# A decoder layer on one core: the sample rows' new SSM states by one product of 96 rounded rows instead of a full fp32 product of 64 rows

## The reference, cut to what matters

```python
xdt = (xs.astype(f32) * dt[..., None]).reshape(bsz, nc, chunk, g, r, p)
bc = bm.astype(f32).reshape(bsz, nc, chunk, g, n)
decay_states = jnp.exp(cs[..., -1:] - cs)
states = jnp.einsum('bcsgn,bgrcs,bcsgrp->bcgrpn', bc, decay_states, xdt)
...
new_states = jnp.einsum('bgrzc,bcgrpn->bzgrpn', decay_chunk, states)
final = new_states[:, -1].reshape(bsz, nh, p, n).astype(h0.dtype)
```

## Time and profile before

| | |
|---|---|
| median of 3 runs | 2976.16 us (2974.51 to 2977.68) |
| the profiled execution | 2979.95 us |
| its span | 2978.2 us |
| TensorE (PE) busy | 2927.1 us, 98% |
| VectorE (DVE) busy | 1876.1 us, 63% |
| ScalarE (ACT) busy | 881.1 us, 30% |
| GpSimd (POOL) busy | 1233.2 us, 41% |
| stage with the scan's steps | about 1770 to 2515 us of the span |

### The profile page before, as it was taken

One profiled execution on the slowest core, in us unless ns is written; L12 is line 12 of the kernel. 1 busy time (PEld: TensorE's weight loads), 2 busy tenths in 40 slices (PEclk: granted clock), 3 DMA queues, 4 the chain that ended last, 5 costly groups with the idle time before them and its releaser, 6 DMA issues.

```text
span 2978.2 us, 51636 instructions
## 1 busy us (share of the span) xinstructions
PE 2927.1 (98%) x22164; PEld 2787.5 (94%) x22164; DVE 1876.1 (63%) x2050; ACT 881.1 (30%) x1411; POOL 1233.2 (41%) x575
## 2 busy tenths in 40 slices
PE   6999999999999999999999999999999999999998
PEld 4898899999999999999999999999999989999886
DVE  3303788898885889979886756686667755111302
ACT  3121222333233333333322233233333343211322
POOL 1133344444433444444444554443444534444332
PEclk9999999999999999999999999999999999999999
DMA  8878886664356886656667666666657665866643
GB/s 330 343 271 336 317 295 240 226 208 152 126 175 209 293 297 228 212 223 255 233 235 272 234 221 215 214 218 242 214 193 242 224 212 194 310 249 236 254 176 141
DMA packets 221035, 704.82 MB, mean 237 GB/s; under 512 B 26932, under 2 KB 130604, under 8 KB 171372
## 3 DMA queue, kind: packets, MB, share of 16 engines
q1 hardware_dynamic: 158262, 471.33, 45.2%
q0 software_dynamic: 5248, 174.60, 14.5%
q10 hardware_dynamic: 57296, 55.59, 5.6%
HBM read 630.85 MB, written 245.17 MB: 294 GB/s over the span
## 4 chain that ended last, share of the span: by engine, by line
PE 92%; DMA 4%; DVE 2%; issue 1%; ACT 0%; SPq 0%; POOL 0%; DVEq 0%; ACTq 0%; POOLq 0%
PE acc L1432 25%; PE acc L1434 24%; PE acc L1433 24%; DMA w_raw<-in_w_in_t 1%; PE ps_s L1301 1%; PE ps_s L1595 1%; DMA w_raw<-in_w_ada_t 1%; PE ps_s L1561 1%; PE ps_t L1446 1%; PE ps_s L1680 1%; PE ps_s L1681 1%; PE ps_s L1682 1%; DMA side<-in_keys_t 1%; PE ps_s L1582 1%; PE acc L1680 0%
## 5 line engine op out<-in xcount | busy, mean ns | idle before, releaser
L921 POOL TENSOR_TENSOR w_lo<-w_raw,w_hi 128x1024 fp32r<-128x1024 f32 (+1 forms) x416 | 1094.5, 2650 | 1697.7 <-ACT w_hi L980 1697.7
L1432 PE MATMUL acc<-act,w_hi 128*128 128x288 f32 x5744 | 1717.8, 299 | 2.7 <-POOL w_lo L921 2.6
L1434 PE MATMUL acc<-act,w_lo 128*128 128x288 f32 x5744 | 1692.9, 295 | 0.0
L1433 PE MATMUL acc<-act,w_hi 128*128 128x288 f32 x5744 | 1692.6, 295 | 0.0
L1432 PEld LDWEIGHTS acc<-act,w_hi 128*128 128x128 f32 x5744 | 1078.9, 188 | 37.2 <-issue 26.8
L1433 PEld LDWEIGHTS acc<-act,w_hi 128*128 128x128 f32 x5744 | 1079.3, 188 | 1.1
L1434 PEld LDWEIGHTS acc<-act,w_lo 128*128 128x128 f32 x5744 | 1078.5, 188 | 0.0
L980 ACT ACTIVATE w_hi<-w_raw 128x1024 fp32r<-128x1024 f32 (+1 forms) x418 | 403.9, 1015 | 482.6 <-PE acc L1434 193.0
L1889 DVE TENSOR_TENSOR side<-side 128x2048 f32<-128x2048 f32 x96 | 274.5, 2859 | 81.9 <-DMA side<-in_vals_t 67.7
L1860 DVE TENSOR_TENSOR side<-side 128x2048 f32<-128x2048 f32 x96 | 269.9, 2811 | 81.2 <-DMA side<-in_keys_t 77.5
L1055 ACT ACTIVATE ev<-acc 128x576 f32<-128x576 f32 x112 | 72.9, 651 | 617.7 <-PE acc L1434 617.5
(11 more groups left out here) (355 smaller groups left out, 2757.8 us busy)
## 6 DMA issues: line engine op xcount, KB each, us to landing
w_raw<-in_w_in_t SPq DMA_DIRECT2D x160, 1024.0 KB, 7.8
out_s_kv<-in_cache_a_w POOLq DMA_DIRECT2D x80, 1632.0 KB, 9.2
side<-in_keys_t SPq DMA_DIRECT2D x52, 1024.0 KB, 7.9
side<-in_vals_t SPq DMA_DIRECT2D x52, 1024.0 KB, 7.9
out_s_kv<-in_cache_a_w POOLq DMA_DIRECT2D x24, 1344.0 KB, 8.1
w_raw<-in_w_ada_t SPq DMA_DIRECT2D x24, 1024.0 KB, 7.4
w_raw<-in_w_gate_t SPq DMA_DIRECT2D x16, 1024.0 KB, 10.2
w_raw<-in_w_o_b_t SPq DMA_DIRECT2D x16, 1024.0 KB, 7.7
```

What stands on the lines that cost most here:

```text
L921: nc.gpsimd.tensor_tensor(dst, raw[:, SLOT[s], ks, 0:cols], wh[:, u % 2, ks, 0:cols].bitcast(F32), ALU.subtract).then_inc(lo, 1)
L1432: nc.tensor.matmul(out, wh[:, c, k, 0:cols], high, start=(k == 0), stop=False)
L1433: nc.tensor.matmul(out, wh[:, c, k, 0:cols], low, start=False, stop=False)
L1434: mm = nc.tensor.matmul(out, wl[:, c, k, 0:cols], high, start=False, stop=(k == kt - 1))
```

## The change

It replaces the fp32 product of 64 rows by one fp32r product of 96 rows for 4 sequences (32 sample rows) at a time. The stationary side `xst` holds three blocks of 32 rows: rounded xds, its rest, rounded xds. The moving side `Bm` (now in `stacked`) holds rounded B, rounded B, rest of B. So one product sums high*high, low*high and high*low.

- ScalarE, step 2: one more copy of the samples' B, rounded, into `B_high`; step 6: a rounded copy of `xds` (32x512) and two 32x256 copies into `xst`, behind a wait on `xe`; step 11: two more 32x256 copies, behind a wait on `sn_t`.
- GpSimd, step 4: two 32x512 operations instead of one 64x1024.
- VectorE, step 5 (nothing stood there): `rows_of_B` (a 64x128 difference and four 32x512 products with the mask) and `sample_inputs` (two 32x256, in place of the 64x256 of step 6); steps 7 and 11: `low_rows`, a 32x256 difference, behind a wait on ScalarE's copies.
- TensorE: the same 32 products in the same places, now with waits on `xst_l` (VectorE's `low_rows`), `bm` and `bd`. `states_new` is called ahead of the other branches of its step, which no other branch shares; its place in the row stays.

```diff
-        Bm = side[0:SAMP, 1920:2944].rearrange("p (b n) -> p b n", b=NB)
+        Bm = stacked[0:96, :].rearrange("p (a b n) -> p a b n", a=2, n=P)
+        xds = side[96:P, 1920:2432].rearrange("p (a h q) -> p a h q", a=2, h=4)
+        xds_high = stacked[96:P, 512:1024].rearrange("p (a h q) -> p a h q", a=2, h=4)
...
+        xst = pairs[0:96, :].rearrange("p (a h q) -> p a h q", a=2, h=2)
+        B_high, B_low = lse[0:SAMP, :].bitcast(F32R), Bt[0:SAMP, 0, :].bitcast(F32R)
...
-                    nc.gpsimd.tensor_tensor(Bm, Bt[0:SAMP, 0, :].unsqueeze(1).broadcast_to((SAMP, NB, P)),
-                                            owner.unsqueeze(2).broadcast_to((SAMP, NB, P)), ALU.mult).then_inc(bm, 1)
-                    pool.wait_ge(bm, g + 1)
+                    for a in range(2):
+                        nc.gpsimd.tensor_tensor(Bm[32 * a:32 * a + 32, a], own_rows(B_high, a).bitcast(F32), own_mask(a), ALU.mult).then_inc(bm, 1)
+                    pool.wait_ge(bm, 2 * g + 2)
...
-                    after(act_e, bm, g)
+                    if i == 0:
+                        after(act_e, bm, 2 * g)
+                        after(act_e, bd, 5 * g)
+                        nc.scalar.activation(B_high, X[0][0:SAMP, 2 * P:3 * P], ACT.Copy)
...
+                if o in (6, 11):
+                    j = o // 11
+                    if j == 0:
+                        act_e.wait_ge(xe, 5 * g + 1)
+                        nc.scalar.activation(xds_high, xds, ACT.Copy)
+                    else:
+                        act_e.wait_ge(sn_t, 4 * g + 2)
+                    for rows in (slice(0, 32), slice(64, 96)):
+                        mm = nc.scalar.activation(xst[rows], xds[:, :, 2 * j:2 * j + 2, :], ACT.Copy)
+                    mm.then_inc(xst_h, 1)
...
-                pe.wait_ge(xe, 5 * g + 1)
-                pe.wait_ge(bm, g + 1)
+                j, half = k // 2, k % 2
+                pe.wait_ge(xst_l, 2 * g + j + 1)
+                pe.wait_ge(bm, 2 * g + 2)
+                pe.wait_ge(bd, 5 * g + 5)
...
-                nc.tensor.matmul(Z, xds[:, 2 * j:2 * j + 2, :].rearrange("p h q -> p (h q)"),
-                                 Bm[:, 4 * half:4 * half + 4, :].rearrange("p b n -> p (b n)"), start=True, stop=True).then_inc(sn_t, 1)
+                nc.tensor.matmul(Z, xst[:, half].rearrange("p h q -> p (h q)"),
+                                 Bm[:, half].rearrange("p b n -> p (b n)"), start=True, stop=True).then_inc(sn_t, 1)
...
+            def sample_inputs(g):
...
+                dve.wait_ge(e4, 5 * g + 1)
+                after(dve, sn_t, 4 * g)
+                for a in range(2):
+                    rows = slice(32 * a, 32 * a + 32)
+                    mm = TT(xds[:, a], xdt[rows, 0], de4[rows, :].unsqueeze(2).broadcast_to((32, 4, 64)), ALU.mult)
+                mm.then_inc(xe, 1)
+
+            def rows_of_B(g):
+
+                dve.wait_ge(bt, 5 * g + 1)
+                TT(B_low, Bt[0:SAMP, 0, :], B_high.bitcast(F32), ALU.subtract).then_inc(bd, 1)
+                after(dve, sn_t, 4 * g)
+                for a in range(2):
+                    TT(Bm[32 * (1 - a):32 * (1 - a) + 32, a], own_rows(B_high, a).bitcast(F32), own_mask(a), ALU.mult).then_inc(bd, 1)
+                dve.wait_ge(bd, 5 * g + 1)
+                for a in range(2):
+                    TT(Bm[64:96, a], own_rows(B_low, a).bitcast(F32), own_mask(a), ALU.mult).then_inc(bd, 1)
+
+            def low_rows(g, j):
+
+                dve.wait_ge(xst_h, 2 * g + j + 1)
+                TT(xst[32:64], xds[:, :, 2 * j:2 * j + 2, :], xds_high[:, :, 2 * j:2 * j + 2, :].bitcast(F32), ALU.subtract).then_inc(xst_l, 1)
...
+                if o == 5:
+                    rows_of_B(g)
+                    sample_inputs(g)
+                if o in (7, 11):
+                    low_rows(g, o // 11)
```

More of the change, by code:

```diff
@@ L404, in h0, with own_rows, own_mask @@
             return buf.rearrange("p (b n) -> p b n", b=NB)
+        def own_rows(rows, a):
+            return rows[32 * a:32 * a + 32].unsqueeze(1).broadcast_to((32, 4, P))
+        def own_mask(a):
+            return owner[32 * a:32 * a + 32, 4 * a:4 * a + 4].unsqueeze(2).broadcast_to((32, 4, P))
         def hT_buf(g, k):
@@ L478, in phase_all @@
         hT_in, h0_in = sems("hT_in0", "hT_in1", "hT_in2"), sems("h0_in0", "h0_in1")
[L479 removed]
+        bm, bd, xst_h, xst_l = sems("bm", "bd", "xst_h", "xst_l")
+        sn_m, sn_t, sn_a, s_out = sems("sn_m", "sn_t", "sn_a", "s_out")
         st_t, st_c, p_out = sems("st_t", "st_c", "p_out")
@@ L1614, in ssm @@
                     products(g, (o - 5) // 2)
-                if o in (8, 10, 14, 16):
-                    states_new(g, (8, 10, 14, 16).index(o))
                 if o in (7, 9, 11, 13, 15):
```

17 lines of the change are left out of this document (8 added, 9 removed).

## The result

The changed kernel takes 2960.46 us (median of 5 runs, 2959.39 to 2969.09) against 2976.16 before: a ratio of 0.995, 95% interval 0.9938 to 0.9961, which is a gain of 11.6 to 18.5 us. The medians differ by 15.7 us where 22.0 were forecast, and the forecast time was 2954.1 us; the time lies inside the range, 0.3 us from that of the rival with a turn missed at step 5 (2960.2). Its profiled execution took 2961.79 us with a span of 2959.8 us.

A forecast was written before the change was run, and what follows sets the result against it. TensorE, busy 98% of the span, was taken as the bound. 29.8 us saved less 5.4 (step 8 stall), 1.4 (copy) and 1.0 (last group) gives 22.0, so 2954.1 us from 2976.16; range 2946.5 to 2962.5.

The forecast's parts named there:

- the rival with a turn missed at step 5: VectorE's last new operation misses w_lo's start; TensorE stalls about 1.0 us in six groups; 2960.2 us, chance 0.2.
- The saving: TensorE's 32 products: 18 save 1.02 us each and 14 save 0.82, together 29.8 us.
- Of this some 0.1 us before and 0.11 us behind it are the change between fp32 and fp32r: Part of the fp32 product's 1.25 us on TensorE, put down to switching type into and out of it.
- the 0.1 us put ahead of the transposes of steps 14 and 16: TensorE, groups but the last: the change of kind moves to the fp32 transposes, so the saving there is 0.82 us.
- the 21.8 us that the Trainium skill's four passes would give: Alternative saving of the 32 products if fp32 costs four passes, 0.91 us each; not adopted.
- The row of seven at step 5: Seven new VectorE operations, 3.3 us, fit before GpSimd's next w_lo with 0.3 us to spare and cost nothing.
- The Trainium skill's rule on quadrants: VectorE, step 5: an instruction beginning in another quadrant waits for earlier ones to finish; the row would take 3.8 us.
- 0 within 0.2 us: GpSimd, step 4: cost of two operations half as wide in place of one.
- The stall of step 8: TensorE waits for VectorE's low_rows, 0.9 us in each of groups 1 to 6, 5.4 us in all.
- The copy at step 2: ScalarE's rounded copy of B delays TensorE's transposes by 0.17 us in 8 groups, 1.4 us.
- Step 6 and step 11: ScalarE's added copies, about 1.2 us and 0.7 us, fit in idle time or delay nothing needed; cost nothing.
- The last group: What the product of step 8 saves there is lost to TensorE's wait for w_lo: 1.0 us.

The follow-up runs named there:

- e5: The kernel before with the product's operands declared rounded (fp32r), still 64 rows, no low parts and no new work; 2960.5 us, ratio 0.9938.
- e9: The kernel before, its product still fp32 but stretched from 64 to 96 rows by zeros written once; 2970.2 us, ratio 0.9970 to before.
- e2: The changed kernel with two of the four 32x512 products of rows_of_B moved from VectorE to GpSimd; 2953.9 us, ratio 0.9918 to before.
- e6: The changed kernel with all four 32x512 products reading rows 32 to 63 and writing rows 64 to 95, values wrong; 2960.3 us, ratio 0.9940 to before.
- e1: The changed kernel with each group's first low_rows moved on VectorE ahead of the older group's reciprocal and scaling; 2962.0 us, ratio 0.9939 to before.
- e8: The changed kernel with all its added work, but its 32 products of 96 rows read as plain fp32; 2981.7 us, ratio 1.0016 to before.
- e3: The changed kernel with ScalarE's rounded copy of B placed behind the plain copy that the transposes need; 2960.2 us, ratio 0.9934 to before.

## Why the prediction was right and where it was wrong

**The saving: right, for a reason partly wrong.** 29.8 us forecast; measured 8 x 3.77 = 30.2, for all 32 products. The product after costs 0.24 us (0.227 forecast). The wrong step is "Of this some 0.1 us before and 0.11 us behind it are the change between fp32 and fp32r": e5 and e9 show that it is the 64 rows, 0.38 us for each product. It did little harm to the sum here, for the change removes both; only the 0.1 us put ahead of the transposes of steps 14 and 16 for a change of kind did not appear (0.37 us in place of 0.46 at step 16 of group 0). I had cost the rows at nothing, and did not see that they were a third of the gain. The total was kept against the 21.8 us that the Trainium skill's four passes would give, because the measured starts decided; that was right.

**The row of seven at step 5: wrong, and as large as the whole miss.** The step that failed is "I take it that the seven fit, with 0.3 us to spare, and cost nothing". Four terms of it went the wrong way: 0.71 us per 32x512 product instead of 0.61 (0.4 us in the row), 0.31 us for the small difference instead of 0.15, 0.43 us between the last two instead of 0.34, and 3.22 us of room instead of 3.51. The rival had the place and the releaser right; by e2 it costs 0.92 us in each of 7 groups, 6.4 us, where 6 x 1.0 were put. That its time fits to 0.3 us (2960.2 against 2960.46) is luck, for the interval of the gain is 7 us wide. The Trainium skill's rule on quadrants (groups of 32 rows) that was named beside it holds (e6), with a price of 0.1 us each. "No row here decides it" was true; with the two outcomes only 0.5 us apart (3.3 and 3.8 us for the row), more of the chance belonged to it than 0.2. **GpSimd: wrong.** "0 within 0.2 us" for two operations half as wide in place of one was 0.25 us by the trace, and it was put down as GpSimd's own affair. It came back on VectorE as 0.25 us less room for the row of seven.

**The stall of step 8: right.** 0.9 us in six groups forecast; recorded 5.7 us in six, by e1 1.07 us each, 6.4. Its mechanism is shown by e1 (a change of VectorE's order alone removes it) and e8 (it doesn't depend on the product). **The copy at step 2: right in time and place**, 0.17 us between the two copies on ScalarE:

```profile
1918.01 0.27 ACT L1157 ACTIVATE lse<-ps_t 64x128 fp32r<-64x128 f32 x1 [8.03 <-DVE side L2226]
1918.18 0.26 ACT L1158 ACTIVATE side<-ps_t 64x128 f32<-64x128 f32 x1
```

It cost 7 x 0.16 = 1.1 us by e3 (1.4 forecast); TensorE's row names 2.2, because half of what it waited for was there already: from the first matrix's transposes to the next one's were 0.64 us before the change and are 0.80 now. **Step 6 and step 11: right at nothing.** There is no wait at steps 10, 13, 14 or 16, and no wait comes from the rounded copies of steps 6 and 11. **The last group: 1.0 forecast**, 0.7 recorded (2.8 instead of 2.1).

The account: 30.2 saved, 6.4 + 6.4 + 1.1 given back, 0.7 more for `w_lo`: 15.6 us, against 15.7 in the medians and 22.0 forecast. The other terms cancel: 0.4 more saved, 1.0 more lost at step 8, 0.3 less at the copy and 0.3 less in the last group. The stage gained 14.8 us because it ends where the last of the 32 products starts, so that product's saving of 1.0 us falls behind it; 15.6 - 1.0 = 14.6.

## What to carry to other kernels

On a kernel that one engine bounds, a saving on that engine arrives whole only if nothing that it reads comes later; look for each new operation at the moment when the shared neighbour (here GpSimd's next `w_lo`) starts, and take a margin of 0.3 us over seven operations for a coin toss, not for cover. Ask too what the change does on that neighbour itself a step earlier: a quarter of a microsecond more on GpSimd was a quarter of a microsecond less room on VectorE. A wait that an order makes can be undone by order alone, without touching the saving: moving two products to GpSimd, one copy behind another and `low_rows` ahead of the reciprocal brought 2946.4 us (2949.9 in the other run of the same kernel); but such a rule must be looked at in the first and last turn of the loop by itself, where the work ahead of it is missing. And before a product is made cheaper by its type, look at its rows: 32 rows of zeros, with no arithmetic changed, took 0.3% off this kernel (0.14 to 0.45%).
